# Hybrid convolution and linear-attention block on 8 cores: transposes moved to the DMA queue one tile earlier, another order of storing weights, early first casts, no drains

## The reference

```
h    = rms_norm(x)
proj = h @ w_in          # c_val, c_gate, c_z, q, k, v, g_lr, g_r, m_conv, m_gla
u    = depthwise_conv31(c_val * sigmoid(c_gate)) + b
yc   = (silu(layer_norm(u)) * silu(c_z)) @ w_conv_out
a    = exp(log_sigmoid(g_lr @ gate_w2 + gate_b) / 16)
o    = gated_linear_attention(q, k, v, a)        # 4 heads, causal
yg   = (rms_norm(o) * silu(g_r)) @ w_gla_out
y    = sigmoid(m_conv) * yc + sigmoid(m_gla) * yg
out  = rms_norm(x + y @ w_out)
```

## Time and profile before

| | |
|---|---|
| median of 3 runs | 1537.07 us (1535.96 to 1540.56) |
| the profiled execution | 1535.22 us, span of its slowest core 1533.7 us |
| spans of the 8 cores | 1520.6 to 1533.7 us |
| busy share of the span | PE 94%, DVE 58%, ACT 41%, POOL 36% |
| DMA issues, all | 152 float32 unit loads, 552 bf16 unit loads, 88 unit stores |

### The profile page before, as it was taken

How to read it: one execution, slowest core, us unless ns; L and a number is a source line. 1 busy time by engine, 2 the same in 40 slices (tenths; PEclk the granted TensorE clock), 3 DMA queues, 4 the chain that set the end, 5 groups by cost and what they waited for, 6 DMA issues and landing times.

```text
span 1533.7 us, 27762 instructions; the slowest of 8 cores (1520.6 to 1533.7 us)
## 1 busy us (share of the span) xinstructions
PE 1442.3 (94%) x8592; PEld 684.7 (45%) x8592; DVE 888.6 (58%) x1264; ACT 633.9 (41%) x1079; POOL 559.7 (36%) x664
## 2 busy tenths in 40 slices
PE   4668998999999999999999999999999999999997
PEld 2223443444544455444544444444544445444543
DVE  2258645676546765478536674376635675376633
ACT  5224844337643365423523353332534254232621
POOL 2116212434224432346224442254424352352523
PEclk9879999999999999999999999999999999999999
DMA  6997998986879779797796959697795958778561
GB/s 209 295 273 236 288 331 293 250 244 213 289 240 257 217 227 316 252 269 226 202 251 187 225 155 257 179 216 203 182 279 188 216 166 225 208 204 218 162 192 56
DMA packets 214639, 348.82 MB, mean 227 GB/s; under 512 B 67424, under 2 KB 100448, under 8 KB 214496
## 3 DMA queue, kind: packets, MB, share of 16 engines
q1 hardware_dynamic: 214352, 346.92, 79.4%
q0 software_dynamic: 144, 0.13, 0.1%
HBM read 259.81 MB, written 39.85 MB: 195 GB/s over the span
## 4 chain that ended last, share of the span: by engine, by line
PE 75%; DVE 6%; DMA 6%; SPq 5%; issue 3%; ACT 2%; POOL 1%; DVEq 0%; POOLq 0%; ACTq 0%
PE ps_pb L423 35%; PE ps_pb L433 13%; PE ps_pb L679 12%; PE ps_pb L834 7%; DMA sb_stg<-w 4%; PE ps_pb L541 4%; SPq L532 3%; DVE sb_U L547 2%; DVE sb_FP L554 1%; DMA sb_wn<-w_b 1%; SPq L378 1%; PE ps_pb L742 1%; PE ps_pb L751 1%; PE ps_pb L746 1%; DMA sb_U<-x 1%
## 5 line engine op out<-in xcount | busy, mean ns | idle before, releaser
L423 PE MATMUL ps_pb<-sb_hT,sb_wn 128*128 128x512 bf16 x2168 | 494.4, 383 | 14.7 <-DVE sb_wn L366 6.9
L423 PEld LDWEIGHTS ps_pb<-sb_hT,sb_wn 128*128 128x128 bf16 x2168 | 212.2, 99 | 268.3 <-issue 29.7
L423 PE MATMUL ps_pb<-sb_hT,sb_stg 128*128 128x512 bf16 x904 | 203.4, 379 | 1.0 <-ACT sb_yb L550 1.0
L679 PE MATMUL ps_pb<-sb_wn,sb_hT 128*128 128x512 bf16 x768 | 180.5, 392 | 23.9 <-ACT sb_wn L369 19.4
L433 PE MATMUL ps_pb<-sb_big,sb_wn 128*128 128x512 bf16 x728 | 168.9, 381 | 0.0
L978 POOL TENSOR_TENSOR sb_yb<-sb_FP 128x512 bf16<-128x512 f32 x64 | 81.1, 1267 | 181.0 <-DVE sb_FP L975 181.0
L423 PEld LDWEIGHTS ps_pb<-sb_hT,sb_stg 128*128 128x128 bf16 x904 | 87.9, 98 | 103.4 <-issue 2.4
L679 PEld LDWEIGHTS ps_pb<-sb_wn,sb_hT 128*128 128x128 bf16 x768 | 76.4, 100 | 123.9 <-issue 40.4
L556 POOL TENSOR_TENSOR sb_FP<-sb_FP,sb_yb 128x512 f32<-128x512 f32 x56 | 73.1, 1305 | 145.6 <-ACT sb_yb L550 145.6
L708 POOL TENSOR_SCALAR sb_Rbf<-sb_Tst,sb_gar 128x256 bf16<-128x256 f32 x128 | 66.7, 538 | 162.4 <-DVE sb_Tst L757 162.4
L589 POOL TENSOR_TENSOR sb_U<-sb_U,sb_FP 128x512 f32<-128x512 f32 x64 | 97.4, 1551 | 56.2 <-DVE sb_FP L575 56.2
(11 more groups left out here) (118 smaller groups left out, 2028.5 us busy)
## 6 DMA issues: line engine op xcount, KB each, us to landing
sb_wn<-w_b SPq DMA_DIRECT2D x354, 256.0 KB, 4.5
sb_stg<-w SPq DMA_DIRECT2D x152, 512.0 KB, 7.9
sb_stg<-w_b SPq DMA_DIRECT2D x198, 256.0 KB, 4.0
sb_big<-sb_u SPq DMA_DIRECT2D x256, 135.0 KB, 7.0
w_b<-sb_wn SPq DMA_DIRECT2D x88, 256.0 KB, 7.9
sb_U<-x SPq DMA_DIRECT2D x36, 512.0 KB, 7.1
out<-sb_U SPq DMA_DIRECT2D x32, 512.0 KB, 5.3
sb_xa<-x SPq DMA_DIRECT2D x28, 512.0 KB, 6.0
```

What stands on the lines that cost most here:

```text
L423: S.op("pe", lambda e, bi=bi, kc=kc, wap=wap: e.matmul(pb[bi][:], lhsT=wap[:, kc * 128:(kc + 1) * 128], rhs=hT[:, hbuf, kc, :], start=(kc ...
L679: S.op("pe", lambda e, bi=bi, kc=kc, s=s, wap=wap: e.matmul(pb[bi][:], lhsT=hT[:, hbuf, kc, s * 128:(s + 1) * 128], rhs=wap[:, (kc % 2) * ...
```

## The change

Five edits. `store_tile` stores the units 40 to 47 in tile 0, with another pattern for the others. The first five casts (all on DVE) are put between the steps that prepare x for tile 0, each followed by the loads for which a staging buffer becomes free. Keys and attention output are transposed by DMA from tile 2 (the third) on, x from tile 3 on (its transposes run in tile 2). The four drains per tile are left out.

```diff
         def store_tile(uid):
-            i = uid - 32
-            if i < 0 or i % 5 in (0, 2):
+            if uid < 24 or 40 <= uid < 48:
                 return 0
-            return 1 if i % 5 == 4 else 2
+            n = uid - 32 if uid < 40 else uid - 40
+            return 0 if n % 3 == 0 else 1 if n % 9 in (1, 4) else 2
...
-        def cast_one(m):
+        def cast_one(m, eng=None):
             i, slot = staged.pop(m), m % NB
+            if eng is None:
+                eng = "dve" if m % 2 == 0 else "act"
...
+        def early_cast():
+            cast_one(pos["cast"], "dve")
+            pos["cast"] += 1
+            while load_one(pos["load"], 0):
+                pos["load"] += 1
...
         def pre_pe(t, s):
-            if t > 3:
+            if t > 2:
                 S.op("sp", lambda e: e.dma_start_transpose(out=hT[:, hbuf, :, s * 128:(s + 1) * 128], in_=hb[:, p, :]),
...
         def gate_in(t):
-            S.op("pe", lambda e: e.drain())
...
-            S.op("pe", lambda e: e.drain())
...
         def gla_a(t, s):
-            for h in range(0 if t >= 3 else 4):
+            for h in range(0 if t >= 2 else 4):
...
         def gla_c(t, s):
-            if t >= 3:
+            if t >= 2:
...
-            S.op("pe", lambda e: e.drain())
             for c in range(8):
                 conv_mm(t, c)
-            S.op("pe", lambda e: e.drain())
...
-            if t >= 3:
+            if t >= 2:
                 for h in range(4):
                     key_t(h)
...
-        for s_ in range(4):
-            pre_sq(0, s_)
-        for s_ in range(4):
-            pre_mul(0, s_)
-            pre_pe(0, s_)
+        pre_sq(0, 0)
+        pre_sq(0, 1)
+        pre_mul(0, 0)
+        pre_mul(0, 1)
+        pre_pe(0, 0)
+        pre_sq(0, 2)
+        pre_mul(0, 2)
+        early_cast()
+        pre_pe(0, 1)
+        pre_sq(0, 3)
+        pre_mul(0, 3)
+        for _ in range(4):
+            early_cast()
+        pre_pe(0, 2)
+        pre_pe(0, 3)
```

More of the change, by code:

```diff
@@ L364, in cast_one @@
                         reads=[B["stg"][i], B["pp"]], writes=[B["wn"][slot]])
-            elif m % 2 == 0:
+            elif eng == "dve":
                 S.op("dve", lambda e: e.tensor_copy(out=wn[:, slot, :], in_=stg[:, i, :]),
@@ L727, in gla_a @@
                 reads=[PB[4], B["maskb"]], writes=[B["atm"][p]])
-            if t < 3:
+            if t < 2:
                 S.op("act", lambda e: e.activation(out=kts[:, s, :], in_=pb6[:, 0:512], func=AF.Copy),
```

## The result

The changed kernel takes **1526.7 us** (median of 15 runs, lowest 1522.6) against 1537.1 for the kernel before, timed on the same chip in turn: a ratio of 0.9927, 95% interval [0.9909, 0.9945]. It is faster by 0.7%. The forecast was 1512.6, 1.6% faster; the time lies inside the range, near its slow end, and 10.4 us are gained where 24.5 were forecast. The profiled execution took 1530.5 us, its slowest core 1528.2.

What follows compares the result with a forecast made beforehand. Tile 0 was taken as waiting for float32 weights, tiles 1 and 2 as 12 and 11 us over the PE-bound steady tile. Terms -8 - 8 - 7 - 1.5 = -24.5 on 1533.7 gave a median of 1512.6 us, range 1503 to 1528.

Steps and rivals of the forecast that it cites:

- Early casts: Start and tile 0: DVE casting all five first units fills the DMA hole and brings the convolution forward; -8 us.
- The bound of -9.2: Better end of the early casts' term: the queue is 9.2 us ahead, the length of the DMA hole.
- the early lead is given back: Rival, tile 0 behind the convolution: PE waits for its own statistics, early casts give only -2, 1518.6 us; chance 0.07.
- Order of stores: Gate projection of tiles 1 and 2: units 40 to 47 read as bf16 remove PE's waits for ACT casts; -8 us.
- The other side: Tile 0: more stores from 122 to 165 us, fewer after; 0 together, ends -2 and +3.
- Drains: Around the convolution and `gate_in` in all eight tiles: leaving out drains saves 0.9 us a tile, -7 us.
- The first rival: Convolution and `gate_in`: the array drains itself at each shape change, drain term only -1, 1518.6 us; chance 0.17.
- Transposes of tile 2: Tile 2: moving them to DMA saves PE 4.4 us, less 3 for late weights; -1.5 us, ends -4.4 and +8.
- 3 us for late weights: Tile 2's later half: cost allowed in the transposes' term for weights delayed by the added DMA time.
- the slower rival: Tile 2: x transposes queue behind float32 loads, ACT waits over 10 us, PE stops; about +30, 1542.6 us; chance 0.03.
- The rival of a DMA-bound later half: Tile 2's later half becomes DMA-bound and costs 12 us instead of 3, 1521.6 us; chance 0.14.
- the prediction's own signs: Profile after: steady tiles about 175 us, tile 2 177 to 180; wrong if `sb_stg` waits pass 5 or span 1528.

Runs made afterwards that it cites:

- e7: e1 with the first casts where they were in the kernel before; 1530.5 us, ratio 0.9924 to the kernel before.
- e5: e1 with the old order of storing weights; 1524.3 us, ratio 0.9882 to the kernel before.
- e1: The changed kernel with all of tile 2's transposes back on PE; 1514.4 us, ratio 0.9844 to the kernel before.
- e6: e1 with the four drains a tile put back; 1527.2 us, ratio 0.9899 to the kernel before.
- e11: The changed kernel with the eight full transposes of tile 2's later half issued on ACT's queue instead of SP's; 1528.6 us, ratio 0.9945.
- e2: The changed kernel with only the x transposes in tile 2 back on PE; 1523.5 us, ratio 0.9914 to the kernel before.
- e3: The changed kernel with only tile 2's attention output transposes back on PE; 1520.7 us, ratio 0.9901 to the kernel before.
- e10: The changed kernel with tile 2's last attention output transpose issued ahead of two loads of x on SP; 1527.1 us, ratio 0.9928.
- e12: The changed kernel with four hb buffers and tile 2's last attention output transpose issued ahead of two x loads; 1522.5 us, ratio 0.9886.
- e4: The changed kernel with four hb buffers for the scaled x instead of two; 1522.8 us, ratio 0.9899 to the kernel before.
- e9: e1 with tile 2's keys and first three of four attention outputs transposed by the queue; 1513.6 us, ratio 0.9843 to the kernel before.

## Why the prediction was wrong, step by step

**Early casts, -8: right, too small.** The five casts of DVE stand where they were put. The first runs at 17.70, and the fifth, whose unit lands at 24.14, ends at 24.92, for the 25.3 that was said; the cast at 27.00 is DVE's sixth, of a unit loaded anew. The second, third and sixth in the kernel after:

```profile
20.45 1.41 DVE L368 CAST sb_wn<-sb_stg 128x1024 bf16<-128x1024 f32 x2
...
27.00 0.70 DVE L368 CAST sb_wn<-sb_stg 128x1024 bf16<-128x1024 f32 x1 [1.50 <-DMA sb_stg<-w]
```

The first stage of tile 0 falls from 42.1 to 29.9 us, its start is 1.3 later (1.5 was said), and nothing behind it is given back; e7 makes the whole 12.3 to 14.6. The bound of -9.2, the length of the hole, was not a bound: the landings show a longer lead. As means of eight cores the 13th float32 unit lands at 44.6 us for 55.6 before, the 81st at 230.6 for 242.3, so the queue is 11 to 12 us ahead from there to the end of tile 0. In the kernel before, PE's waits for casts from 29 to 140 us were, in that first stage (L423),

```profile
PE ps_pb L423 <- DVE sb_wn L366: 6.9, 2, 6.4
PE ps_pb L423 <- ACT sb_wn L369: 5.5, 2, 4.0
```

12.4 us, not only the 6.42 of the earlier trace rows; after, there is no such row of L431. (In v, which follows, they stay as they were: 15.5 us before, 15.3 after.) On that core (7) the first stage took 44.8 us, 17.2 more than the 27.6 of tile 1: 12.4 of waits, the rest at a lower clock (granted 0.89 from 27.8 to 69.9 us, 1.00 in the same stage after). As the mean of eight cores the stage had lost 42.1 - 27.6 = 14.5 us and now loses 2.3. The rival "the early lead is given back" is refuted.

**Order of stores, -8: right.** PE now goes through the gate projection of tiles 1 and 2 without a pause, 13.8 us each on every core from its first matmul to the next stage, for 17.4 and 17.7 before (mean; 16.6 to 18.6):

```profile
337.27 13.98 PE L685 MATMUL ps_pb<-sb_wn,sb_hT 128*128 128x512 bf16 x64
...
523.61 13.98 PE L685 MATMUL ps_pb<-sb_wn,sb_hT 128*128 128x512 bf16 x64
```

That is 7.5 us, less than the 9.3 read from core 7, one of the slower ones. e5 gives 5.8 to 8.0 for the whole. The other side was put at 0 with ends of its own, and some of it shows: the attention stage of tile 1 takes 37.1 us for 36.3 on the mean, so tile 1 fell to 185.8, and to 184.4 in e1, where about 182 was forecast.

**Drains, -7: right, a little small.** Around the convolution in tile 3 and `gate_in` in tile 5 of the kernel after:

```profile
686.45 1.03 PE L685 MATMUL ps_pb<-sb_wn,sb_hT 128*128 128x512 bf16 x4
687.40 14.00 PE L549 MATMUL ps_pb<-sb_big,sb_wn 128*32 128x512 bf16 x256
701.33 3.63 PE L431 MATMUL ps_pb<-sb_hT,sb_wn 128*128 128x512 bf16 x16
...
1056.88 0.81 PE L578 MATMUL ps_pb<-sb_HP,sb_onesb 128*128 128x512 bf16 x3
1057.88 0.38 PE L578 MATMUL ps_pb<-sb_HP,sb_onesb 128*128 128x512 bf16 x1 [0.19 <-DVE sb_HP L571]
1058.10 4.26 PE L431 MATMUL ps_pb<-sb_hT,sb_wn 128*128 128x512 bf16 x19
...
1150.56 5.34 PE L441 MATMUL ps_pb<-sb_big,sb_stg 128*128 128x512 bf16 x24
1155.84 0.61 PE L625 MATMUL ps_pb<-sb_hT,sb_wglr 128*32 128x512 bf16 x8
1156.38 3.63 PE L840 MATMUL ps_pb<-sb_stg,sb_yb 128*128 128x512 bf16 x16
```

By the prediction's own way of counting, the gaps are now 687.40 - 687.32 = 0.08, 701.33 - 701.22 = 0.11, 0.10 and 0.11 us, together 0.40 for 1.89: 1.49 gone, where half was expected to stay. And DVE holds PE as said: at 1057.88 PE is 0.35 us behind four matmuls in a row. 1.49 - 0.35 = 1.14 a tile, 9.1 for eight tiles, for the 0.9 and 7 of the forecast; the steady tiles went from 176.2 to 175.0, and e6 gives 8.5 to 9.5 for the whole. The first rival, the array that drains itself at each change of shape for most of the old gap, is refuted by this: the gap that this trace shows at such a change, without a drain instruction, is 0.1 us. By the Trainium skill, TensorEngine Tiling (Array Packing), Key Properties, a change of the tiling mode drains TensorE; if it does, this trace leaves no more than the 0.1 us for it.

**Transposes of tile 2, -1.5: this is the step that failed.** It measured about +12, outside its own ends (-4.4 to +8). The rest came as forecast in sum: -8 - 8 - 7 = -23, and e1 is 24 us faster than before (0.9844). There is some luck in that. The casts gave 4 us or more beyond their term, and the three parts undone one by one come to 26.6 us by the ratios and 32.1 by the last matmuls, more than the 24 of all three together; intervals of 4 to 6 us each don't tell whether they overlap. Two things were wrong in the transposes' term.

First, I compared amounts over the half tile: 13 us of added transfers against 17 us of room. The amounts were about right. e11 gives the price of one, since there six of them have a queue of their own: 9.5% of 90 us are 8.6 us, 1.4 a transpose (1.5 to 1.8 was said). By the Trainium skill, DMA: Bandwidth & Descriptors, Latency and other measured facts, 256 KB at 261 GB/s would take 1.0 us, as an estimate. The row above differs from it and decides. But room somewhere in the half tile is no room where they are wanted. The share from 600 to 632 us was 1.01 before, a row that the prediction itself quoted; e1 shows the stage full and PE not waiting.

Second, I priced what would be late as weights, "3 us for late weights", with a lead of 10 us and up to five staged loads. In e1 the weights had lead enough. The transposes had next to none: PE is through with all that is ahead of the last attention output at 582.25, 4.8 us after the issue of its transpose begins, and goes on at 590.31, 12.9 us after it; ACT gets its hb buffer 11.8 us after the issue of the first x transpose begins (590.28 to 602.13). In tile 3 these land in 4.4 and 3.4 us. PE's wait for the attention output (8.1 us, 8.8 in e2) stood in no term and no rival. ACT's wait did, in the slower rival: it said 16 us twice, with the point at 10, and the first is 15.7, the second 8.3. It had a chance of 0.03, because the casts run 10 us ahead. What it left out is DVE: L491 waits for ACT's square, and behind L491 stand both L965, which frees PE's bank and has no such lead (the 4.0 us of the timeline above), and DVE's casts, whose lead is used up after a wait of 13 to 14 us (e3, e10). So the rival is right as to the late landing, ACT's wait and the stop of PE behind it. Its price of 30 counted both waits in full, where the second stayed below its point; its reason, the place behind float32 loads in the queue, fell with e11. The rival of a DMA-bound later half had the right cause. Its victim, the weights, was late only in part (v of tile 2, and e12), and its 12 us were too few: with the 4.4 that PE saves in tile 2, the +12 measured are 16 lost.

That each kind costs 8 to 9.5 us and both 13, and which waits carry it, is shown by e2, e3, e4, e10 and e12. Two things were not tried. One is taking float32 loads out of tile 2 itself; tile 3, with the same transposes and no such loads, takes 41.7 us, but it also has ten more bf16 slots. The other is putting L965 and the casts ahead of L491 in DVE's program, which by the timeline should take PE's second wait away.

Of the prediction's own signs, the steady tiles fell to 175.0 as forecast and no wait for a staging buffer's load passed 5 us (the longest is ACT's 4.9), but the span came out at 1528.2, just above the 1528 that it had named, and tile 2 at 193.3 for 177 to 180.

## What to carry to other kernels

Before work is moved to the DMA queues, look at the share in the very stage, and ask of each transfer how long before its use it is issued: in this kernel prefetched weights bore a full set of engines, and a transfer issued when its data was ready and wanted some microseconds later cost 8 us or more. Ask too what stands behind the waiting instruction on each engine: ACT's wait reached PE through DVE, which runs its program in order. Put only those that have a lead, or fall into a stage with room, on the queue (e9), and leave the last ones before a consumer on the compute engine. A hole in the supply of weights can cost more than its length: the 9.2 us without loads at the start cost 12 us of the first stage (e7), in waits and at a lower granted clock.

## What the runs showed of the hardware that I had not expected

A DMA transpose of 256 KB is issued in 1.2 us when the queue runs light, and holds the issuing engine for 7.4 to 7.6 us where the queue is full of weight loads (DMA share 1.16 from 571.6 to 600 us; up to 8.5 on another core, 9.4 in e4), while plain DMAs around it are issued in 0.3 to 0.6 us. From 600 to 630 us, at a share of 0.86, the next three take 1.3 to 1.6. On another, otherwise empty queue the issue takes 1.6 us at the same load and the landing 11 to 15 (medians): a second queue frees the issuing engine, not the transfer. A change between 128x128 and 128x32 tiles of TensorE costs 0.1 us without a drain instruction, 0.4 to 0.5 with one.
